# Row rotations by on-chip transfers, a projection tile moved ahead of the indexer, and three smaller edits to a two-layer encoder

## The reference, cut to what matters

```python
h = layer_norm(DN_ALPHA * h + 0.5 * swiglu(h, gate0, up0, down0), ln_g[0], ln_b[0])
o, state = mixer(h)        # p = h @ w_in ; rope on qa, ka, qb, kb, qi, ki ; attention A, B, C, D ; @ w_o
h = layer_norm(DN_ALPHA * h + o, ln_g[1], ln_b[1])
h = layer_norm(DN_ALPHA * h + 0.5 * swiglu(h, gate1, up1, down1), ln_g[2], ln_b[2])
# rope: x * cos + (the other half of the head, signed) * sin
# indexer: score = sum_h relu(qi_h . ki) * w_h ; the best keys of it are kept for attention B
```

## Time and profile before

| what | value |
|---|---|
| median of three runs | 1152.07 us (1151.99 to 1152.39) |
| the profiled execution's own time | 1151.99 us |
| span of it, first to last instruction | 1150.2 us |
| PE busy | 1132.4 us (98%) |
| DVE, ACT, POOL busy | 684.9, 541.5, 86.4 us |
| granted TensorE clock, mean | 1.00 |

### The profile page before, as it was taken

One profiled execution on the slowest core, in us unless ns is written; L12 is line 12 of the kernel. 1 busy time (PEld: TensorE's weight loads), 2 busy tenths in 40 slices (PEclk: granted clock), 3 DMA queues, 4 the chain that ended last, 5 costly groups with the idle time before them and its releaser, 6 DMA issues.

```text
span 1150.2 us, 20743 instructions
## 1 busy us (share of the span) xinstructions
PE 1132.4 (98%) x8616; PEld 1099.7 (96%) x8616; DVE 684.9 (60%) x929; ACT 541.5 (47%) x770; POOL 86.4 (8%) x84
## 2 busy tenths in 40 slices
PE   9999999999999999999999999999999999999998
PEld 8999999978899999999999999999788989999997
DVE  6545445778659754545585544467777596454443
ACT  6343443464755634344373434345547565344332
POOL 1000000100161000000100000010003310000001
PEclk9999999999999999999999999999999999999999
DMA  9554444432433545444445544443433425444431
GB/s 346 184 178 151 173 146 159 165 128 91 152 114 117 211 149 182 148 163 165 148 149 189 175 157 162 165 151 117 166 109 132 150 79 216 158 171 154 159 126 42
DMA packets 28788, 178.20 MB, mean 155 GB/s; under 512 B 3568, under 2 KB 3632, under 8 KB 11056
## 3 DMA queue, kind: packets, MB, share of 16 engines
q1 hardware_dynamic: 26976, 171.36, 43.6%
q0 software_dynamic: 1744, 5.88, 1.5%
HBM read 171.79 MB, written 4.25 MB: 153 GB/s over the span
## 4 chain that ended last, share of the span: by engine, by line
PE 88%; DVE 7%; ACT 3%; issue 2%; DMA 0%; SPq 0%; ACTq 0%; DVEq 0%
PE ps L505 26%; PE ps L507 26%; PE ps L506 26%; ACT w_high L1136 2%; DVE z L1626 1%; DVE w_low L1465 1%; DVE w_low L1478 1%; PE ps L795 1%; PE ps L952 1%; PE ps L953 1%; PE ps L954 1%; DVE z L1616 1%; DVE zx_low L1606 1%; DVE x_low L1641 1%; PE ps L910 1%
## 5 line engine op out<-in xcount | busy, mean ns | idle before, releaser
L505 PE MATMUL ps<-x_high,w_high 128*128 128x288 f32 x1536 | 455.5, 297 | 3.9 <-DVE w_low L1465 3.1
L507 PE MATMUL ps<-x_high,w_low 128*128 128x288 f32 x1536 | 453.1, 295 | 0.0
L506 PE MATMUL ps<-x_low,w_high 128*128 128x288 f32 x1536 | 453.1, 295 | 0.0
L1465 DVE TENSOR_TENSOR w_low<-raw,w_high 128x2048 fp32r<-128x2048 f32 (+3 forms) x150 | 326.6, 2180 | 208.8 <-ACT w_high L1136 208.5
L1136 ACT ACTIVATE w_high<-raw 128x2048 fp32r<-128x2048 f32 (+2 forms) x166 | 302.6, 1827 | 113.8 <-PE ps L507 107.7
L505 PEld LDWEIGHTS ps<-x_high,w_high 128*128 128x128 f32 x1536 | 288.4, 188 | 8.3 <-issue 3.9
L507 PEld LDWEIGHTS ps<-x_high,w_low 128*128 128x128 f32 x1536 | 288.5, 188 | 0.0
L506 PEld LDWEIGHTS ps<-x_low,w_high 128*128 128x128 f32 x1536 | 288.3, 188 | 0.1
L505 PE MATMUL ps<-hid_high,w_high 128*128 128x288 f32 x704 | 208.4, 296 | 0.0
L506 PE MATMUL ps<-hid_low,w_high 128*128 128x288 f32 x704 | 208.0, 295 | 0.0
L507 PE MATMUL ps<-hid_high,w_low 128*128 128x288 f32 x704 | 207.9, 295 | 0.0
(11 more groups left out here) (318 smaller groups left out, 1143.2 us busy)
## 6 DMA issues: line engine op xcount, KB each, us to landing
raw<-weights SPq DMA_DIRECT2D x138, 1024.0 KB, 4.9
raw<-weights SPq DMA_DIRECT2D x16, 768.0 KB, 4.3
raw<-weights SPq DMA_DIRECT2D x4, 968.0 KB, 4.7
raw<-weights SPq DMA_DIRECT2D x6, 512.0 KB, 4.1
raw<-weights SPq DMA_DIRECT2D x8, 256.0 KB, 6.2
out_k<-kT POOLq DMA_DIRECT2D x2, 864.0 KB, 4.5
raw<-weights SPq DMA_DIRECT2D x2, 640.0 KB, 5.5
hT<-x_in SPq DMA_DIRECT2D x4, 288.0 KB, 5.5
```

The costliest lines, as they stand in the source:

```text
L505: pe.matmul(out, wh, xh, start=first, stop=False, skip_group_check=True)
L506: pe.matmul(out, wh, xl, start=False, stop=False, skip_group_check=True)
L507: return pe.matmul(out, wl, xh, start=False, stop=last, skip_group_check=True)
L1465: dve.tensor_tensor(wl, r, wh.bitcast(F32), ALU.subtract).then_inc(low_ready, 1)
```

## The change

Six edits, in the diff's order.

- EARLY_FFN goes from 1 to 2. For n = 0, 2 and 3 DVE adds the last tile to `zsum` and its square to `zsqsum`, and PE makes one matmul for the mean and one for the squares.
- Tile 3 of a feed-forward network gets PSUM bank 2, and its wait for `early_read` goes.
- The matmul permutations of rotations 0 and 1 go. `turn_rows` on SP makes them, ahead of the load of M5, into `relu_l` (0) and `cq_x` (1). DVE makes both cosine products, then `w_low` of M4, then both sine products.
- Tile 4 goes between `sample_tokens` and the indexer's products, and `sample_logits(1, 0)` behind tile 5. ACT's list in the mixer stays as it is.
- For n = 0 and 3 DVE makes `w_low` of M2 in two halves, the second after tile 3 of the norm.
- For n = 1, 2 and 4 ACT rounds chunk 3 before the last x tile instead of after it, and DVE makes its `w_low` at the start of `early_gate`.

```diff
-EARLY_FFN, EARLY_MIX = 1, 2
+EARLY_FFN, EARLY_MIX = 2, 2
...
         def gate_bank(t):
-            return (0, 6, 4)[t % 3]
+            return 2 if t == 3 else (0, 6, 4)[t % 3]
...
+                        if local == TM_AT + NRAW:
+                            turn_rows(l, 0)
+                            turn_rows(l, 1)
...
-                    pe.wait_ge(early_read, early_before(event - 1) + 1)
...
                 mean, square = stat_banks(n)
                 pe.wait_ge(zsum_ready, n + 1)
+                if sums_whole(n):
+                    pe.matmul(mean, ones, zsum[:, 0, :], start=True, stop=True).then_inc(mean_ready, 1)
+                    pe.wait_ge(all_squares_ready, whole_before(n) + 1)
+                    pe.matmul(square, ones, zsqsum[:, 0, :], start=True, stop=True).then_inc(stat_ready, 1)
+                    for k in range(first, KD):
+                        early_tile(n, k)
+                    return
...
-            def swap(l, r, bank):
-                pe.wait_ge(proj_copied, TILES * l + ROPES[r][0] + 2)
-                for j in range(2):
-                    mm = pe.matmul(ps[:, bank + j, 0:TOK], swap_a, rope_x[:, r % 2, j, :], start=True, stop=True)
-                mm.then_inc(swapped, 1)
...
-                    if k % 4 == 0:
+                    if k == 0:
+                        pe.wait_ge(half_low_ready, early_before(event - 1) + 1)
+                    if k in (2, 4):
                         pe.wait_ge(low_ready, l * LAYER_CHUNKS + TM_AT + k // 4 + 1)
...
-                    if t == 4:
+                    if t == 5:
                         pe.wait_ge(relu_ready, 3 * l + 2)
                         sample_logits(1, 0)
-                    if t == 5:
                         key_rotation(l)
...
-                    if k == 5:
-                        swap(l, 0, SWAP_AT[0])
-                swap(l, 1, SWAP_AT[1])
                 sample_tokens()
+                project_tile(2, 0)
                 indexer_second_block(l)
                 indexer_first_block(l)
                 pe.wait_ge(v_parts_copied, l + 1)
                 pe.matmul(ps[0:32, TM_BANK[2], 0:V_TOK], add_four, v_parts, start=True, stop=True).then_inc(v_added, 1)
-                for i in range(2, FM_CHUNKS):
-                    project(i)
+                project_tile(2, 1)
+                for i in range(3, FM_CHUNKS):
+                    for j in range(len(FM_TILES[i])):
+                        project_tile(i, j)
...
-                        if which == 0 and j == 3:
+                        if j == (3 if which == 0 else 6):
                             high_until(next_chunks(n) + NSPLIT + 1)
...
                 def early_gate():
                     n = 3 * l + 2 * i - 1
+                    low_until(base + 1 + NSPLIT)
                     dve.wait_ge(chunk_used, base + 1)
...
                     dve.wait_ge(early_read, early_before(n) + 1)
-                    low_until(base + 1 + NSPLIT)
...
+                    if at_ == 7 and sums_whole(n):
+                        dve.wait_ge(z_ready, 5 * (n + 1))
+                        dve.tensor_tensor(zsum[:, 0, :], zsum[:, 0, :], z[:, 7, :], ALU.add).then_inc(zsum_ready, 1)
+                        dve.wait_ge(zsqsum_ready, n + 1)
+                        dve.wait_ge(zsq_ready, 5 * (n + 1))
+                        dve.tensor_tensor(zsqsum[:, 0, :], zsqsum[:, 0, :], zsq[:, 1, :], ALU.add)\
+                            .then_inc(all_squares_ready, 1)
...
-                if n in EARLY and which == 0:
-                    low_until(next_chunks(n) + NSPLIT)
-                if n in EARLY and which > 0:
+                if n in EARLY:
                     low_half(next_chunks(n) + 2, 0, half_low_ready)
...
-                    if n in EARLY and which > 0 and j == 4:
+                    if n in EARLY and j == (3 if which == 0 else 4):
                         low_half(next_chunks(n) + 2, 1)
...
                 rope_first(l, 0)
                 fixed_choice()
+                rope_first(l, 1)
+                low_until(base + 5)
                 rope_rest(l, 0)
-                rope_first(l, 1)
                 rope_rest(l, 1)
-                low_until(base + 5)
                 indexer(l, 0)
```

More of the change, by code:

```diff
@@ L102 @@
 WO_ROW = {"A": 0, "B": 1, "C": 2, "D": 3}
-SWAP_AT = (0, 4)
-BY_PE = 3
 D_SWAP = 1
@@ L266, in encoder_program @@
         half_ready, proj_copied = sem("half_ready"), sem("proj_copied")
-        swapped, rows_turned = sem("swapped"), sem("rows_turned")
+        swapped = sem("swapped")
+        rows_turned = [sem(f"rows_turned{parity}") for parity in range(2)]
         roped = sem("roped")
@@ L311, in gate_bank, with turned, turned_count, sums_whole @@
         def gate_bank(t):
-            return (0, 6, 4)[t % 3]
+            return 2 if t == 3 else (0, 6, 4)[t % 3]
         def down_bank(q):
             return (6, 4)[q % 2]
-        turned = relu_l[:, 0:2 * TOK].rearrange("p (j t) -> p j t", j=2)
+        def turned(r):
+            return cq_x[:, :, :] if r == 1 else relu_l[:, 0:2 * TOK].rearrange("p (j t) -> p j t", j=2)
+        def turned_count(l, r):
+            return 4 * 16 * (2 * l + r // 2 + 1)
         def last_bank(j):
             return (0, 1, 6, 7, 4)[j - BY_DVE]
-        def ffn_before(n):
-            return sum(m % 3 > 0 for m in EARLY if m < n)
+        def sums_whole(n):
+            return n in EARLY and n % 3 != 1
+        def whole_before(n):
+            return sum(sums_whole(m) for m in range(n))
         def squares_added(n, q):
@@ L400, in turn_rows @@
                     other = b + 1 - 2 * (b % 2)
-                    sp.dma_start(turned[32 * b:32 * b + 32], rope_x[32 * other:32 * other + 32, r % 2, :, :])\
-                        .then_inc(rows_turned, 16)
+                    sp.dma_start(turned(r)[32 * b:32 * b + 32], rope_x[32 * other:32 * other + 32, r % 2, :, :])\
+                        .then_inc(rows_turned[r % 2], 16)
             for pair in range(4):
@@ L967, in sample_tokens, with project_tile @@
                     mm.then_inc(v_parts_ready, 1)
-                def project(i):
+                def project_tile(i, j):
                     wh, wl = weights_of(i)
-                    pe.wait_ge(low_ready, l * LAYER_CHUNKS + fm_local(i) + 1)
-                    for j, t in enumerate(FM_TILES[i]):
-                        if t == 5:
[L975 to L982, removed]
+                    t = FM_TILES[i][j]
+                    if j == 0:
+                        pe.wait_ge(low_ready, l * LAYER_CHUNKS + fm_local(i) + 1)
+                    if t == 5:
+                        pe.wait_ge(values_copied, 3 * (l + 1))
+                    if t > 5:
+                        pe.wait_ge(proj_copied, TILES * l + t - 1)
+                    for k in range(KD):
+                        mm = three(ps[:, tile_bank(t), 0:TOK], wh[:, j, k, :], wl[:, j, k, :], x_high[:, k, :],
+                                   x_low[:, k, :], k == 0, k == KD - 1)
+                    mm.then_inc(chunk_used if t == FM_TILES[i][-1] else half_ready, 1)
+                    after_tile(t)
                 def after_tile(t):
-                    if t == 4:
+                    if t == 5:
                         pe.wait_ge(relu_ready, 3 * l + 2)
                         sample_logits(1, 0)
-                    if t == 5:
                         key_rotation(l)
@@ L1568, in residual @@
                         dve.wait_ge(z_ready, 5 * n + 4)
-                        dve.tensor_tensor(zsum[:, 0, :], zsum[:, 0, :], z[:, 6, :], ALU.add).then_inc(zsum_ready, 1)
+                        ins = dve.tensor_tensor(zsum[:, 0, :], zsum[:, 0, :], z[:, 6, :], ALU.add)
+                        if sums_whole(n):
+                            link(ins)
+                        else:
+                            ins.then_inc(zsum_ready, 1)
+                    if at_ == 7 and sums_whole(n):
[5 more added lines that the diff above has]
+                            .then_inc(all_squares_ready, 1)
                 zq = z[:, 2 * q:2 * q + 2, :]
@@ L1690, in key_rotation, with rope_cos @@
                 dve.tensor_tensor(kr_t[:, :, 1, :], kr_a[:, :, 1, :], kr_b[:, :, 1, :], ALU.add).then_inc(kr_roped, 1)
+            def rope_cos(r):
+                return qn[:, :, :] if r == 1 else rope_a[:, :, :]
             def rope_first(l, r):
                 dve.wait_ge(proj_copied, TILES * l + ROPES[r][0] + 2)
-                link(dve.tensor_tensor(rope_a[:, :, :], rope_x[:, r % 2, :, :],
+                link(dve.tensor_tensor(rope_cos(r), rope_x[:, r % 2, :, :],
                                        tab[:, 0, 1:2, :].to_broadcast([P, 2, TOK]), ALU.mult))
             def rope_rest(l, r):
[L1700 to L1706, removed]
+                dve.wait_ge(rows_turned[r % 2], turned_count(l, r))
+                link(dve.tensor_tensor(rope_b[:, :, :], turned(r),
                                        tab[:, 1, 1:2, :].to_broadcast([P, 2, TOK]), ALU.mult))
```

13 lines of the change are left out of this document (7 added, 6 removed).

## The result

The changed kernel takes 1160.26 us (median of four runs, 1159.16 to 1161.27), against 1152.03 for the kernel before on the same chip: ratio 1.0070 [1.0057, 1.0083]. It is slower, as forecast, but by 8.2 us where 3.9 were forecast, and it lies above the range. Its profiled execution is the run of 1159.16, 7.2 above the profiled execution of before.

The account below looks back on a forecast made before the run. The prediction took PE, busy for 98% of the span, to bound the kernel. It added 3.3 us for two mixers and 0.65 for the starts of networks to 1151.99, giving 1155.9 us; range 1153.2 to 1159.0.

Parts of the forecast that it names:

- the sum of 3.9: Whole kernel: 3.3 us from two mixers plus 0.65 from the starts of networks, slower than before; chance 0.70.
- Indexer forecast at 249.2: First layer's mixer: the indexer's first matmul starts at 249.2, 0.9 us later than before, set by transfers and DVE.
- Wait before tile 5: Mixer: with tile 4 gone from there, PE waits 0.7 us for ACT's copy of the sample values.
- Wait before tile 6: Mixer: PE idles 4.3 us instead of 0.9 for w_low of M5, in both layers.
- Tile 6 forecast 1.6 later: Mixer: tile 6 starts 1.6 us later than before, everything behind it follows; +3.3 over two layers.
- Starts of networks: After norms 1, 2 and 4: chunk 4 and so tile 4 come 0.2 us later, three times; +0.65 taken.
- the bounds that the terms state: Whole kernel: the terms' bounds were said to give 1154.0 to 1157.7 us, without the transfers' far end.
- the clock falls in the 4.3 us wait: Rival, before tile 6: slow matmuls follow, 2.5 us more once or twice, 1158.4 or 1160.8; chance 0.10.
- Later waits: Rival, behind tile 6: the wait for ACT's latent statistics absorbs the delay, 2.3 us back, 1153.6; chance 0.12.
- The transfers were not slow: Rival, rotations in the mixer: slow transfers cost 3.9 us more in each layer, 1163.7; chance 0.03.
- The faster case: Rival, before tile 6: its wait stays 0.9 us, w_high of M5 before the last indexer product, 1149.1; chance 0.05.

Follow-up runs that it names:

- e9: The kernel before with only the reordered starts of networks after norms 1, 2 and 4, and tile 3 in bank 2 without its waits: 1152.98 us.
- e1: The changed kernel with eight matmuls whose result nobody reads, put behind tile 5 into the wait before tile 6: 1156.17 us.
- e2: The changed kernel with w_high of M5 before ACT's last relu and its w_low before DVE's second indexer step: 1148.21 us.
- e3: The changed kernel with tile 4 back behind the indexer's products and the last indexer product behind it, transfers kept: 1158.51 us.
- e10: The changed kernel with four matmuls whose result nobody reads behind tile 5, filling part of the wait before tile 6: 1156.45 us.

## Why the prediction was wrong

**What held.** The direction, and the sum of 3.9 term by term. Indexer forecast at 249.2, measured 249.15. Wait before tile 5 forecast 0.7, measured 0.65. Wait before tile 6 forecast 4.3, measured 4.31. Tile 6 forecast 1.6 later, measured 1.57 and 1.45. Starts of networks forecast 0.65 in all, measured 0.28, 0.29 and 0.26; e9 shows the first of them alone. One sum was wrong: the bounds that the terms state give about 1152.3 to 1156.2, not 1154.0 to 1157.7. The measured time lies outside either. The transfers cost nothing that the forecast had not: the second four start at 242.41, and their landing holds DVE for 0.33. e1 gives the same sum as a time, 1156.17 for 1155.9.

**The step that failed** is the price of the 4.3 us wait. The sum took the wait at its own length and put a fall of TensorE's clock in it at nothing; the fall stood among the rivals (*the clock falls in the 4.3 us wait*) with a chance of 0.10. It happened in both layers, and the prediction's own sign of it, matmuls behind tile 6 at twice their distance, is there. The rival's price was near: 1160.8 was worked out for two falls, 1160.26 was measured; a fall took 2.05 by the medians, for 2.5. e1 shows that the idle time caused it: with the wait filled, the clock stays at its full level.

What was wrong is the weighing. The sentence against the rival was that the clock column shows 1.00 in the first stretch, so that the slow passes of the earlier trace rows might be something else. But at the start of an execution the column is no evidence: in e9 it shows 1.00 from 6 to 11 us, while the matmuls there stand 0.24 apart, the distance that they have at 0.51 in the changed kernel. The slow pace was the evidence, and the column was believed instead. And "no run here shows that", written of a fall in idle time, was not so. The trace of the kernel before shows one at its end: the timeline of PE has its last matmul, and the view by stretch has the clock some three us later.
```profile
1145.63 0.65 PE L625 MATMUL ps<-minus_mean,mat 128*128 128x288 f32 x2
```
```profile
1149.00:1150.00 1.00, 0.00 (x0) 0.00 (x0) 0.00 (x0) 0.00 (x0) 0.00 (x0) 0.59 0.32 122
```
It costs nothing there, as no matmul follows. But it shows the clock of the kernel before falling within 4 us of PE's last work, and a wait of 4.3 was forecast.

The rule that the prediction set beside the wait is that of the Trainium skill (TensorE: Matmul & The Clock Gate, Part 1: The HAM clock gate): an idle array falls back to 1.2 GHz until sustained work releases it. The trace of the changed kernel agrees, with 0.51 of full speed behind the wait and 1.00 from 266 on.

**The range** went up to 1159.0, for one of two falls. But the two layers run the same lists and open the same wait of 4.31, so a fall in one made a fall in the other likely, and the range had to take in 1160.8 or leave the clock out altogether. That both fall was not certain: in the second layer the clock fell only just before the wait ended (the last section has the rows).

**The other rivals.** Later waits did not take it up: ACT's latent statistics hold PE for 2.3 in two, as before. The transfers were not slow. The faster case did not occur; e2 shows that it was one line of ACT's list and one of DVE's away.

## What to carry to other kernels

When an edit leaves PE with a wait longer than any through which the trace shows the clock held, price the wait and the matmuls behind it at half clock, once for every repetition of the stage. Look for a long idle stretch of PE in the trace at hand, its end included, before saying that there is no row for it. A piece of PE work that is moved forward leaves a hole where it stood: move with it the rounding of the chunk that it covered, on every engine that prepares it. Where the hole can't be closed, matmuls whose result nobody reads were cheaper than the hole here (e1).

## What the runs showed that was not expected

- The clock falls inside the wait, not behind it: the stretch 244 to 249 of e3, in which PE does almost nothing, has a mean granted clock of 0.81, and the first matmuls behind it run at 0.51. Where in the wait it falls differs between equal waits: in the changed kernel the stretch 258 to 260 of the first layer is at 0.78 already, but the stretch 830 to 832 of the second, which lies later in its wait, is still at 1.00, and the fall comes in the 0.75 us before tile 6 starts at 832.75.
```profile
258.00:260.00 2.00, 0.00 (x0) 0.00 (x0) 0.70 (x1) 2.00 (x2) 0.00 (x0) 0.78 0.02 4
830.00:832.00 2.00, 0.00 (x0) 0.00 (x0) 1.60 (x1) 2.00 (x2) 0.00 (x0) 1.00 0.00 0
832.00:834.00 2.00, 1.25 (x5) 1.25 (x6) 2.00 (x2) 2.00 (x3) 0.00 (x0) 0.64 0.16 27
```
- Waits of 4.31 (after the change) and 4.65 (e3) lowered it; one of 2.18 (e10), with four matmuls of filler ahead of it, kept 1.00 in the one execution that has a trace.
- The price differs between equal waits of one execution: 18 slow matmuls in the first layer, 12 in the second. The four runs of the changed kernel spread over 2.1 us, those of before beside them over 0.4. That the clock's return makes this spread was not tested, and part of any spread comes from elsewhere: fifteen later runs of before (those beside e9) spread over 1.7, and e9's profiled execution lost its 1.47 at the start of the execution.
